# Norms in an fp32 kernel of two transformer blocks: token sums as columns, small reciprocals, TensorE turning them into rows

## The chip, the core and the metric

The kernel runs on one core of a Trainium2 chip. The metric is the device time of one execution in microseconds (us); the runs of the kernel before give 1356.03 us as their median.

## What is computed

Two blocks run one after the other on 256 tokens of 1024 features, all in float32. The first has two layers (FFN, mixer, FFN; the mixer is a short convolution in one and a three-branch attention in the other, with shared keys and values). The second has an even mixer (sparse attention and retention) and an odd mixer (differential and latent attention), each with a pre-norm and a post-norm. What the change touches is the root mean square norm, over the 1024 features of a token or over the 64 or 128 features of one head:

```python
def rms_norm(x, gain=None):
    xf = x.astype(jnp.float32)
    y = xf * lax.rsqrt(jnp.mean(xf * xf, axis=-1, keepdims=True) + NORM_EPS)
    if gain is not None:
        y = y * gain.astype(jnp.float32)
    return y.astype(x.dtype)

def head_group_norm(x):
    mu = jnp.mean(xf, axis=-1, keepdims=True)
    var = jnp.mean(jnp.square(xf - mu), axis=-1, keepdims=True)
    return ((xf - mu) * lax.rsqrt(var + NORM_EPS)).astype(x.dtype)
```

Such norms stand ahead of every FFN, mixer and projection (eight of them over 1024 features are touched), on the queries of the first attention (16 heads of 64), on the retention output (4 heads of 128, `head_group_norm`), on the differential attention output (4 heads of 128), and behind both mixers of the second block (post-norms).

## The kernel before

**Layout.** Activations lie with features on the 128 partitions and the 256 tokens along the free axis: `hres` holds the residual as 8 tiles of 128x256. One core runs everything; each engine has its own program, written by hand in the order in which it executes, and the engines meet at semaphores. A wait on an engine holds all that stands behind it there.

**Products.** Every large product is three TensorE matmuls (`mm3`, L744 to L746): weights and activations are each split into a high and a low fp32r part. Weights arrive in chunks (`raw_a`); ScalarE writes the high part (`hi_a`, L1225), VectorE the low part (`lo_a`, L1692, 128x2048 for a full chunk). The second matrix of an FFN, mixer or convolution comes by rows through `raw_b`, whose low part GpSimd makes (`low_quarters`, L2328, four 128x256 pieces a row tile).

**Deferred norm.** A stage does not wait for its norm. ScalarE writes the gained residual tiles (`gained`) and TensorE runs the first weight chunk on them (`first_chunk`, L733 to L738). Meanwhile ScalarE squares the residual, two tiles an instruction, into `sqm` (`square_residual`, L1319). `sum_pairs` (L713) then adds the eight 128x256 tiles of squares over partitions with a matrix of ones as stationary operand, so that every partition holds the sum of each token as a row of 256. ScalarE takes the root (`root_pairs`, L1341), VectorE inverts it (`inverse_rms`, L1682, 128x256) into `rln`, and the products are scaled by it when they leave PSUM. In a projection `turn_rms` (L723, two one-column matmuls after the second job) also turns it into a column per token half, `rtok`, for outputs with tokens on partitions.

**Order of work around the norms.** In a projection (`project`), job after job fills bank 4 or 5; after job 0 TensorE does the sum, and `between(c)` runs small extra work after chunk c. On ScalarE a chunk's end is followed by the high part of chunk c+2, then by `between(c)`; on VectorE by the scaling of the job, the low part of chunk c+2, then `between(c)`. At chunk 0 VectorE makes the low part of chunk 2 first and inverts after it. The even projection has 16 jobs, one a chunk; its `between` on VectorE holds the top-64 selection (`best`, rounds of MAX and MATCH_REPLACE) at chunks 8, 9, 11 and 12.

**Head norms.** `sum_squares` (L690) is one 512-column matmul of `sqs` against ones or `blk1` (ones in two 64x64 blocks), with rows as a result again. The inversion is of 128x512: in the q projection for two query pairs (L1675), inside the first attention in four pieces of 128x256 (`late_queries`, L2108), after the even attention (`group_root`, L2156) and after the odd attention (`c_norm`, L2292).

**Post-norms.** `post_residual` (from L1763): the four banks are squared by ScalarE, folded from 8 tiles to 4 by VectorE (L1770), summed by TensorE (`sum_residual`, L702), rooted (L1299), inverted (L1675) and multiplied in (L1783, or L1777 for the last one).

**Attention.** `attend` is a pipeline over pairs of heads: TensorE scores, VectorE maximum and bias, ScalarE exponential, VectorE and GpSimd scaling, TensorE transposes (L949 to L954) and values (L968 to L976). `mix_out` multiplies by the output matrix in `OUT_ORDER`; for the odd mixer the tiles of the second half come first.

## Time and profile before

| | us |
|---|---|
| median of 3 runs | 1356.03 (1355.47 to 1356.52) |
| span of the profiled execution, first to last instruction | 1354.7 |
| TensorE busy in it | 1302.7 (96%) |
| VectorE busy | 831.3 (61%) |
| ScalarE busy | 614.4 (45%) |
| GpSimd busy | 502.5 (37%) |

The page gives the profiled execution by its span; its own device time is not listed apart from the runs, whose median lies 1.3 us above the span. The mean granted TensorE clock is 0.980 of full speed. A matmul's listed duration contains its latency, so durations of matmuls that follow each other overlap: what one costs is read from the distance between starts. An fp32 matmul is listed as two instructions (x2), an fp32r one as one. ScalarE is ACT, VectorE DVE, GpSimd POOL, TensorE PE in the rows; "[0.74 <-ACT wah L1225]" means that the engine sat idle for 0.74 us until that line on that engine released it.

### The profile page before, as it was taken

The numbers are of one execution on the slowest core, as the hardware profiler recorded it, in microseconds if no ns is written. First come the engines' busy times: TensorE is split into PE (matmuls) and PEld (weight loads), VectorE is DVE, ScalarE is ACT, GpSimd is POOL, SyncE is SP. The second block draws the span as 40 slices with busy tenths as digits, with TensorE's granted clock in tenths as the row PEclk, the third lists the DMA queues.
The fourth block names the chain that finished last, engine by engine and source line by source line (L and its number), as shares of the span: only waits on it lengthen the run. The fifth ranks groups of instructions, "written<-read, shape, count | busy, mean of one in ns | idle before, by whom it ended". The sixth has DMA issues, their size and how long they took to land.

```text
span 1354.7 us, 27623 instructions
## 1 busy us (share of the span) xinstructions
PE 1302.7 (96%) x10767; PEld 1247.2 (92%) x10767; DVE 831.3 (61%) x1353; ACT 614.4 (45%) x880; POOL 502.5 (37%) x533
## 2 busy tenths in 40 slices
PE   8999999999999998999999889999999998989978
PEld 6999999999999998999999668999999997889768
DVE  4775557786555566554455785755556685875576
ACT  5444435344443345433335576534434346443382
POOL 2655443325444524455540244444442001700043
PEclk9999999999999998999998889999999999989989
DMA  8787754666776556666653114566653444334400
GB/s 257 211 234 220 219 171 141 187 187 207 228 231 187 171 162 176 199 186 187 197 160 129 56 48 130 173 200 197 199 177 121 156 139 181 112 95 133 148 32 32
DMA packets 275121, 222.61 MB, mean 164 GB/s; under 512 B 8098, under 2 KB 256438, under 8 KB 274924
## 3 DMA queue, kind: packets, MB, share of 16 engines
q1 hardware_dynamic: 272528, 215.59, 52.1%
q0 software_dynamic: 1504, 4.49, 1.7%
q10 hardware_dynamic: 1020, 1.58, 0.3%
q8 instruction: 47, 0.77, 0.2%
q14 instruction: 22, 0.18, 0.0%
HBM read 216.40 MB, written 4.19 MB: 163 GB/s over the span
## 4 chain that ended last, share of the span: by engine, by line
PE 83%; DVE 9%; ACT 4%; issue 1%; DMA 1%; POOL 1%; DVEq 0%; SPq 0%; ACTq 0%; POOLq 0%
PE psum L744 24%; PE psum L746 23%; PE psum L745 23%; PE psum L713 2%; PE psum L733 1%; PE psum L734 1%; DVE wal L1885 1%; PE psum L738 1%; DVE wal L1692 1%; ACT wah L1225 1%; PE psum L928 1%; DVE hn_tiles L1746 1%; ACT pbuf L1491 1%; DVE rstd L1675 1%; DVE hn_tiles L1745 1%
## 5 line engine op out<-in xcount | busy, mean ns | idle before, releaser
L744 PE MATMUL psum<-hn_tiles,wah 128*128 128x256 f32 x2032 | 570.4, 281 | 4.5 <-DVE wal L1692 2.4
L2328 POOL TENSOR_TENSOR wbl<-raw_b,wbh 128x256 fp32r<-128x256 f32 x412 | 402.0, 1005 | 465.6 <-ACT wbh L1232 443.0
L745 PE MATMUL psum<-hn_tiles,wah 128*128 128x256 f32 x2032 | 563.4, 277 | 0.0
L746 PE MATMUL psum<-hn_tiles,wal 128*128 128x256 f32 x2032 | 563.1, 277 | 0.0
L744 PEld LDWEIGHTS psum<-hn_tiles,wah 128*128 128x128 f32 x2032 | 382.4, 188 | 9.7 <-issue 4.7
L745 PEld LDWEIGHTS psum<-hn_tiles,wah 128*128 128x128 f32 x2032 | 381.9, 188 | 1.9 <-issue 1.7
L746 PEld LDWEIGHTS psum<-hn_tiles,wal 128*128 128x128 f32 x2032 | 382.1, 188 | 0.0
L1692 DVE TENSOR_TENSOR wal<-raw_a,wah 128x2048 fp32r<-128x2048 f32 (+3 forms) x127 | 288.9, 2274 | 111.5 <-ACT wah L1225 110.7
L1225 ACT ACTIVATE wah<-raw_a 128x2048 fp32r<-128x2048 f32 (+2 forms) x125 | 235.3, 1884 | 69.2 <-PE psum L746 54.9
L1351 ACT ACTIVATE gate_hid<-tmp 128x256 f32<-128x256 f32 x88 | 36.7, 417 | 415.3 <-DVE tmp L1802 415.3
L744 PE MATMUL psum<-hidh,wbh 128*128 128x256 f32 x768 | 212.6, 277 | 0.9 <-DVE hidl L1746 0.9
L745 PE MATMUL psum<-hidl,wbh 128*128 128x256 f32 x768 | 212.2, 276 | 0.0
L746 PE MATMUL psum<-hidh,wbl 128*128 128x256 f32 x768 | 212.1, 276 | 0.0
L1802 DVE TENSOR_TENSOR tmp<-psum,rms 128x512 f32<-128x512 f32 x88 | 60.8, 691 | 215.6 <-PE psum L746 208.7
L2397 POOL TENSOR_SCALAR pbuf<-pbuf,rs 128x256 f32<-128x256 f32 x36 | 35.8, 1004 | 319.5 <-DVE rs L1947 244.7
L744 PEld LDWEIGHTS psum<-hidh,wbh 128*128 128x128 f32 x768 | 144.2, 188 | 1.3 <-DVE hidl L1746 1.3
L746 PEld LDWEIGHTS psum<-hidh,wbl 128*128 128x128 f32 x768 | 144.2, 188 | 0.0
L745 PEld LDWEIGHTS psum<-hidl,wbh 128*128 128x128 f32 x768 | 144.2, 188 | 0.0
L1232 ACT ACTIVATE wbh<-raw_b 128x1024 fp32r<-128x1024 f32 x96 | 100.2, 1044 | 10.5 <-PE psum L746 6.1
L1806 DVE TENSOR_TENSOR gate_hid<-gate_hid,tmp 128x256 f32<-128x256 f32 x88 | 39.1, 444 | 43.6 <-ACT gate_hid L1351 43.6
L733 PE MATMUL psum<-hn_tiles,wah 128*128 128x256 f32 x144 | 40.2, 314 | 7.9 <-ACT hn_tiles L1305 4.3
L1746 DVE TENSOR_TENSOR hidl<-gate_hid,hidh 128x256 fp32r<-128x256 f32 x96 | 43.4, 452 | 3.4 <-DVE hidh L1745 0.2
(303 smaller groups left out, 1646.1 us busy)
## 6 DMA issues: line engine op xcount, KB each, us to landing
raw_a<-in_ffn_w_in SPq DMA_DIRECT2D x176, 512.0 KB, 5.0
raw_b<-in_ffn_w_out SPq DMA_DIRECT2D x88, 512.0 KB, 4.3
raw_a<-in_w_in_even SPq DMA_DIRECT2D x15, 1024.0 KB, 5.2
raw_a<-in_conv_w_in SPq DMA_DIRECT2D x24, 512.0 KB, 4.3
raw_a<-in_w_in_odd SPq DMA_DIRECT2D x11, 1024.0 KB, 5.2
raw_a<-in_w_kv SPq DMA_DIRECT2D x6, 1024.0 KB, 5.0
raw_b<-in_conv_w_out SPq DMA_DIRECT2D x8, 512.0 KB, 5.6
raw_a<-in_attn_w_q SPq DMA_DIRECT2D x4, 1024.0 KB, 5.3
```

Of the source, the lines that this page charges most:

```text
L733: mm(dst, wh, hnh[:, k, :], start=k == 0 and i == 0, stop=False)
L744: mm(dst, wh, xh, start=start, stop=False)
L745: mm(dst, wh, xl, start=False, stop=False)
L746: return mm(dst, wl, xh, start=False, stop=stop)
L1225: act.activation(wah[:, s, :, 0:w], raw_a[:, wa.slot(u), :, 0:w], ACT.Copy).then_inc(S("a_hi"), 1)
L1232: act.activation(wbh[:, s], raw_b[:, s], ACT.Copy).then_inc(S("b_hi"), 1)
L1351: act.activation(silu[:, gs, :], tmp[:, gs, 0:T], ACT.Silu).then_inc(S("silu_ready"), 1)
L1692: v.tensor_tensor(wal[:, s, :, 0:w], raw_a[:, (n["ra"] + u) % 2, :, 0:w], wah[:, s, :, 0:w].bitcast(F32), ALU.subtract).then_inc(S("a_lo"), 1)
L1746: return v.tensor_tensor(xl, x, xh.bitcast(F32), ALU.subtract)
L1802: v.tensor_tensor(tmp[:, gs, :].rearrange("p (g c) -> p g c", g=2), bank[4 + gs][:, :].rearrange("p (g c) -> p g c", g=2), rln[:, None, :] ...
L1806: link(v.tensor_tensor(hf[:, hs, :], silu[:, gs, :], tmp[:, gs, T:2 * T], ALU.mult))
L2328: x = g.tensor_tensor(low[:, c], full[:, c], high[:, c].bitcast(F32), ALU.subtract)
```

## The change

- **Token sums as columns.** `sum_tokens` makes the squares the stationary operand and one column of ones the moving one: per tile two fp32 matmuls with a one-column result, tokens on partitions. Eight tiles are folded to four before it, for the deferred norms by GpSimd (`fold_squares`).
- **Small roots.** ScalarE takes the root of 128x2, 128x4 or 128x8 (`rtt`), VectorE inverts as little (`token_roots`, `head_roots`). For tokens the result is `rtok` directly, and `turn_rms` with its copy goes.
- **Back to rows.** `rms_row` (two fp32 matmuls) and `head_rows` (four or eight) take the inverted column, broadcast over the free axis, as stationary operand and the identity as moving one; the rows land in PSUM. TensorE issues them after the twelfth matmul (k == 4) of the next job: in an FFN of the second chunk, in the convolution of its third group, in a projection of job 1; for heads of a later job (`amid`). VectorE copies the token rows to `rln`, or reads head rows from PSUM directly, and then signals `row_taken`, for which later TensorE work waits.
- **Head norms moved.** The late queries are scaled at attention steps 1 and 2; the retention norm is done at chunks 12 to 14 of the even projection instead of after the attention; the odd one at attention steps 10 and 11 and after it.

```diff
-def sum_residual():
-    pe.wait_ge(S("rt_ready"), n["rn"])
-    for j in range(4):
-        n["half"] += 1
-        pe.wait_ge(S("half_ready"), n["half"])
-        m = mm(bank[6][:, 0:T], one1, sqm[:, 2 * j, :], start=j == 0, stop=j == 3)
+def sum_tokens(b, tiles, ready):
+    pe.wait_ge(S("row_taken"), n["row"])
+    for j, t in enumerate(tiles):
+        ready(j)
+        for tt in range(2):
+            m = mm(b[:, tt:tt + 1], sqm[:, t, tt * P:(tt + 1) * P], one1[:, 0:1],
+                   start=j == 0 and tt == 0, stop=j == len(tiles) - 1 and tt == 1)
     m.then_inc(S("ss_ready"), 1)
     n["rn"] += 1
-    n["sqn"] += 4
+def half_tiles(j):
+    n["half"] += 1
+    pe.wait_ge(S("half_ready"), n["half"])
+def fold_tiles(j):
+    n["fold"] += 1
+    pe.wait_ge(S("fold_ready"), n["fold"])
+def sum_residual():
+    pe.wait_ge(S("rt_ready"), n["rn"])
+    sum_tokens(bank[6], range(0, KT, 2), half_tiles)
 def sum_pairs():
     pe.wait_ge(S("rt_ready"), n["rn"])
-    for j in range(4):
-        pe.wait_ge(S("sqn_ready"), n["sqn"] + j + 1)
-        for t in (2 * j, 2 * j + 1):
-            m = mm(bank[7][:, T:2 * T], one1, sqm[:, t, :], start=t == 0, stop=t == KT - 1)
+    sum_tokens(bank[7], range(0, KT, 2), fold_tiles)
+def rms_row(b):
+    n["tok"] += 1
+    pe.wait_ge(S("tok_ready"), n["tok"])
+    for tt in range(2):
+        m = mm(b[:, T + tt * P:T + (tt + 1) * P], rtok[:, tt:tt + 1].to_broadcast([P, P]), ident,
+               start=True, stop=True)
+    m.then_inc(S("row_ready"), 1)
+    n["row"] += 1
+def sum_head_tokens(b, src, per_tile):
+    n["sq"] += 1
+    pe.wait_ge(S("sq_ready"), n["sq"])
+    pe.wait_ge(S("row_taken"), n["row"])
+    col = halves2 if per_tile == 2 else one1[:, 0:1]
+    for t in range(2):
+        for tt in range(2):
+            c = per_tile * (2 * t + tt)
+            m = mm(b[:, c:c + per_tile], src[:, t * T + tt * P:t * T + (tt + 1) * P], col,
+                   start=True, stop=True)
     m.then_inc(S("ss_ready"), 1)
     n["rn"] += 1
-    n["sqn"] += 4
-def turn_rms():
-    n["tok"] += 1
-    pe.wait_ge(S("rms_ready"), n["tok"])
-    for tt in range(2):
-        m = mm(bank[7][:, T - 2 + tt:T - 1 + tt], rln[:, tt * P:(tt + 1) * P], ident[:, 0:1],
-               start=True, stop=True)
-    m.then_inc(S("tok_ready"), 1)
+def head_rows(b, slot, per_tile):
+    n["hrow"] += 1
+    pe.wait_ge(S("rh_ready"), n["hrow"])
+    for t in range(2):
+        for tt in range(2):
+            c = per_tile * (2 * t + tt)
+            w = P // per_tile
+            for j in range(per_tile):
+                m = mm(b[w * j:w * (j + 1), t * T + tt * P:t * T + (tt + 1) * P],
+                       rh[:, slot, c + j:c + j + 1].to_broadcast([P, w]), ident, start=True, stop=True)
+    m.then_inc(S("row_ready"), 1)
+    n["row"] += 1
...
+                if sums and i is FIRST and u == 1 and g == 0 and k == 4:
+                    rms_row(bank[7])
...
+                if i is FIRST and u == 0 and k == 4:
+                    rms_row(bank[7])
...
+                    if part == 0 and k == 4:
+                        rms_row(bank[7]) if idx == 1 else amid(idx)
...
+    pe.wait_ge(S("row_taken"), n["row"])
...
+    elif c == 1:
+        sum_squares(1, 60, blk1)
     else:
-        sum_squares(1, 60 if c == 1 else 512, blk1)
-project("q", q_between)
+        pe.wait_ge(S("rt_ready"), n["rn"])
+        sum_head_tokens(bank[6], sqs, 2)
+project("q", q_between, lambda idx: head_rows(bank[6], idx % 2, 2) if idx >= 3 else None)
 pe.wait_ge(S("nsa_in"), 1)
 pe.wait_ge(S("swap_kT"), 32)
 def nsa_between(st):
     if st == 1:
-        sum_squares(1, 512, blk1)
+        head_rows(bank[6], 1, 2)
+        sum_head_tokens(bank[7], sqs, 2)
+    elif st == 2:
+        head_rows(bank[7], 0, 2)
     elif st == 3:
-        pe.wait_ge(S("rt_ready"), n["rn"])
-    elif st in (12, 15, 18, 21):
-        pe.wait_ge(S("late_queries"), st // 3 - 3)
+        pe.wait_ge(S("row_taken"), n["row"])
...
-        sum_squares(1, 512, one1)
-project("even", even_between)
+        pe.wait_ge(S("rt_ready"), n["rn"])
+        sum_head_tokens(bank[6], sqs, 1)
+project("even", even_between, lambda idx: head_rows(bank[idx - 11], idx % 2, 1) if idx in (13, 14) else None)
 wait_scaled(pe, PJ["even"])
 wait_finished(pe, PJ["even"])
 pe.wait_ge(S("dsa_in"), 1)
 attend("even")
 mix_out("even")
 sum_residual()
+rms_row(bank[6])
...
-        sum_squares(1, 512, one1, (sqs[:, :], rstd[:, :])[st - 9], bank[st - 9])
+        sum_head_tokens(bank[st - 9], (sqs, rstd)[st - 9], 1)
+    if st == 11:
+        head_rows(bank[0], 0, 1)
 attend("odd", sum_heads)
+head_rows(bank[1], 1, 1)
 mix_out("odd")
 sum_residual()
+rms_row(bank[6])
...
+def head_roots(b, w, inv):
+    act.wait_ge(S("ss_ready"), n["rn"] + 1)
+    act.wait_ge(S("rt_used"), n["rn"])
+    act.activation(rtt[:, 0:w], b[:, 0:w], ACT.Sqrt, bias=eps[:, 0:1], scale=inv
                    ).then_inc(S("rt_ready"), 1)
     n["rn"] += 1
...
-def inverse_rms(tokens=False):
+def token_roots():
     v.wait_ge(S("rt_ready"), n["rn"] + 1)
-    link(v.reciprocal(rln, rt[:, 0:T]))
+    link(v.reciprocal(rtok, rtt[:, 0:2]))
     v.sem_inc(S("rt_used"), 1)
-    if tokens:
-        v.sem_inc(S("rms_ready"), 1)
+    v.sem_inc(S("tok_ready"), 1)
+    n["rn"] += 1
+def inverse_rms():
+    token_roots()
+    n["row"] += 1
+    v.wait_ge(S("row_ready"), n["row"])
+    link(v.tensor_copy(rln, bank[7][:, T:2 * T]))
+    v.sem_inc(S("row_taken"), 1)
+def head_roots(slot, w):
+    v.wait_ge(S("rt_ready"), n["rn"] + 1)
+    link(v.reciprocal(rh[:, slot, 0:w], rtt[:, 0:w]))
+    v.sem_inc(S("rt_used"), 1)
+    v.sem_inc(S("rh_ready"), 1)
     n["rn"] += 1
...
-    inverse_root(T)
+    token_roots()
+    n["row"] += 1
+    v.wait_ge(S("row_ready"), n["row"])
+    row = rstd[:, 0:T]
+    link(v.tensor_copy(row, bank[6][:, T:2 * T]))
+    v.sem_inc(S("row_taken"), 1)
...
 def normed_queries(j):
-    inverse_root(512)
+    n["row"] += 1
+    v.wait_ge(S("row_ready"), n["row"])
     qq = qT[:, 2 * j:2 * j + 2, :].rearrange("p t c -> p (t c)")
-    link(v.scalar_tensor_tensor(qq, qq, gq[:, 0:1], rstd[:, :], ALU.mult, ALU.mult))
+    link(v.scalar_tensor_tensor(qq, qq, gq[:, 0:1], bank[6 + j // 3][:, :], ALU.mult, ALU.mult))
+    v.sem_inc(S("row_taken"), 1)
 def q_between(c):
     if c == 1:
         inverse_root(60)
         link(v.scalar_tensor_tensor(kcT[:, :], kcT[:, :], gk[:, 0:1], rstd[:, 0:60], ALU.mult, ALU.mult))
-    elif c in (2, 3):
-        normed_queries(c - 2)
+    elif c in (2, 3, 4):
+        head_roots((c + 1) % 2, 8)
+        if c < 4:
+            normed_queries(c - 2)
 project("q", q_between)
 wait_finished(v, PJ["q"])
 def late_queries(st):
-    if st in (6, 9, 12, 15):
-        j, t = 2 + (st - 6) // 6, (st // 3) % 2
-        if t == 0:
-            v.wait_ge(S("rt_ready"), n["rn"] + 1)
-        link(v.reciprocal(rstd[:, 0:T], (rt if j == 2 else sqs)[:, t * T:(t + 1) * T]))
-        x = v.scalar_tensor_tensor(qT[:, 2 * j + t, :], qT[:, 2 * j + t, :], gq[:, 0:1], rstd[:, 0:T],
-                                   ALU.mult, ALU.mult)
-        link(x)
-        v.sem_inc(S("late_queries"), 1)
-        if t == 1:
-            v.sem_inc(S("rt_used"), 1)
-            n["rn"] += 1
+    if st == 1:
+        normed_queries(2)
+        head_roots(0, 8)
+    elif st == 2:
+        normed_queries(3)
...
 def group_norm(j):
     r2 = bqk[:, 2 * j:2 * j + 2, :].rearrange("p t c -> p (t c)")
     g2 = bg[:, 2 * j:2 * j + 2, :].rearrange("p t c -> p (t c)")
-    link(v.tensor_tensor(r2, r2, rstd[:, :], ALU.mult))
+    n["row"] += 1
+    v.wait_ge(S("row_ready"), n["row"])
+    link(v.tensor_tensor(r2, r2, bank[2 + j][:, :], ALU.mult))
+    v.sem_inc(S("row_taken"), 1)
     link(v.tensor_tensor(r2, r2, g2, ALU.mult))
...
     elif c == 12:
         best(0, range(HALF, 2 * HALF))
+        head_roots(1, 4)
+    elif c == 13:
+        wait_finished(v, PJ["q"] + 8)
+        group_norm(0)
+        head_roots(0, 4)
+    elif c == 14:
+        group_norm(1)
 project("even", even_between)
 wait_finished(v, PJ["even"])
 v.sem_inc(S("dsa_in"), 1)
-attend("even", behind=lambda st: group_root(0) if st == len(STAGES["even"]) else None)
+attend("even")
 for j in range(2):
-    if j:
-        group_root(j)
-    group_norm(j)
...
+def c_scaled(j):
+    n["row"] += 1
+    v.wait_ge(S("row_ready"), n["row"])
+    link(v.scalar_tensor_tensor(pair(cq, j), pair(cq, j), gsub[:, 0:1], bank[j][:, :], ALU.mult, ALU.mult))
+    v.sem_inc(S("row_taken"), 1)
+def c_gated(j):
+    link(v.scalar_tensor_tensor(pair(cq, j), pair(cq, j), 1.0 - LAM_INIT, pair(cg, j), ALU.mult, ALU.mult))
     for t in (2 * j, 2 * j + 1):
         x = split(hnh[:, t, :], hnl[:, t, :], cq[:, t, :])
     x.then_inc(S("tile_ready"), 1)
-attend("odd")
+def c_norm(st):
+    if st in (10, 11):
+        head_roots(st - 10, 4)
+    if st == 11:
+        c_scaled(0)
+attend("odd", behind=c_norm)
+c_scaled(1)
 for j in range(2):
-    c_norm(j)
+    c_gated(j)
...
+def fold_squares():
+    for j in range(4):
+        g.wait_ge(S("sqn_ready"), n["sqn"] + j + 1)
+        g.tensor_tensor(sqm[:, 2 * j, :], sqm[:, 2 * j, :], sqm[:, 2 * j + 1, :], ALU.add
+                        ).then_inc(S("fold_ready"), 1)
+    n["sqn"] += 4
```

The first place is VectorE at chunks 12 to 15 of the even projection, before the change (`L2175`, `L2176`, `L2179` and `L2180` are the last rounds of `best`, `wal` the low part of a chunk, `arena<-psum,rms` the scaling of a job):

```order
L2175 MAX top<-arena 128x8 [waits dve_link]
L2176 MATCH_REPLACE arena<-top,arena 128x128 [waits dve_link]
L2179 TENSOR_SCALAR arena<-arena 128x128 [waits dve_link]
L2180 TENSOR_TENSOR arena<-arena,cst 128x128 [waits dve_link]
L1692 TENSOR_TENSOR wal<-raw_a,wah 128x2048 [waits a_hi,dve_link]
L1736 TENSOR_TENSOR arena<-psum,rms 128x512 [waits a_lo,pj_ready]
L1736 TENSOR_TENSOR arena<-psum,rms 128x512 [waits pj_ready]
```

and after it:

```order
L2248 MAX top<-arena 128x8 [waits dve_link]
L2249 MATCH_REPLACE arena<-top,arena 128x128 [waits dve_link]
L2252 TENSOR_SCALAR arena<-arena 128x128 [waits dve_link]
L2253 TENSOR_TENSOR arena<-arena,cst 128x128 [waits dve_link]
L1757 RECIPROCAL rh<-rtt 128x4 [waits rt_ready,dve_link]
L1766 TENSOR_TENSOR wal<-raw_a,wah 128x2048 [waits dve_link,a_hi]
L2235 TENSOR_TENSOR arena<-arena,psum 128x512 [waits a_lo,row_ready,job_finished]
L2237 TENSOR_TENSOR arena<-arena 128x512 [waits dve_link]
L1757 RECIPROCAL rh<-rtt 128x4 [waits rt_ready,dve_link]
L1810 TENSOR_TENSOR arena<-psum,rms 128x512 [waits dve_link,pj_ready]
```

The small reciprocal stands behind the selection, and the first scaling by head rows (L2235) and the second reciprocal behind the low part of the last chunk.

The second place is TensorE there, after the change: the end of job 12, the sum of chunk 12 (L747), twelve matmuls of job 13 (two rows of the twelve shown last), then the head rows (L761), and, 36 matmuls later, the sum of chunk 13:

```order
L785 MATMUL psum<-wah,hn_tiles 128x256
L747 MATMUL psum<-cst,sqs 128x1 [waits row_taken,sq_ready,rt_ready]
L747 MATMUL psum<-cst,sqs 128x1 x3
L783 MATMUL psum<-wah,hn_tiles 128x256 [waits job_scaled,a_lo]
...
L784 MATMUL psum<-wal,hn_tiles 128x256
L785 MATMUL psum<-wah,hn_tiles 128x256
L761 MATMUL psum<-cst,rh 128x128 [waits rh_ready]
L761 MATMUL psum<-cst,rh 128x128 x3
L783 MATMUL psum<-wah,hn_tiles 128x256
...
L747 MATMUL psum<-cst,sqs 128x1 [waits row_taken,sq_ready,rt_ready]
```

Before, one L690 stood for each sum, and nothing in job 13 or 14 waited for VectorE's reciprocals.

The third place is VectorE at the end of the odd attention after the change (L2066 multiplies a head pair by its gate, L1819 and L1820 split it, L2373 is the scaling by head rows):

```order
L1757 RECIPROCAL rh<-rtt 128x4 [waits rt_ready]
L2066 TENSOR_TENSOR arena<-psum,arena 128x256 [waits dve_link,job_finished,pv_done]
L1819 CAST hn_tiles<-arena 128x256 [waits o_evac]
L1820 TENSOR_TENSOR hn_tiles<-arena,hn_tiles 128x256 [waits dve_link]
L1757 RECIPROCAL rh<-rtt 128x4 [waits rt_ready]
L2373 SCALAR_TENSOR_TENSOR arena<-arena,par,psum 128x512 [waits dve_link,row_ready]
L2066 TENSOR_TENSOR arena<-psum,arena 128x256 [waits dve_link,job_finished,pv_done]
L1819 CAST hn_tiles<-arena 128x256 [waits o_evac]
L1820 TENSOR_TENSOR hn_tiles<-arena,hn_tiles 128x256 [waits dve_link]
L2373 SCALAR_TENSOR_TENSOR arena<-arena,par,psum 128x512 [waits row_ready]
```

Before, both reciprocals (of 128x512) and both scalings stood behind the last split, and `mix_out` did not wait for them; now its first matmul waits for `row_taken`, the signal behind the last L2373.

## Rows read from the trace of the kernel before

**Rows 1.** Share and count of each engine's busy time (page, part 1)

```profile
PE 1302.7 (96%) x10767; PEld 1247.2 (92%) x10767; DVE 831.3 (61%) x1353; ACT 614.4 (45%) x880; POOL 502.5 (37%) x533
```

**Rows 2.** TensorE timeline, kv projection: start us, us, engine line op out<-in xcount

```profile
487.37 3.62 PE L713 MATMUL psum<-arena,cst 128*128 128x256 f32 x16
...
490.64 0.47 PE L744 MATMUL psum<-hn_tiles,wah 128*128 128x256 f32 x1
```

**Rows 3.** Groups by line, TensorE: xcount | busy us, mean ns | idle before

```profile
L1202 PE MATMUL psum<-cst,arena 128*128 128x128 f32 x32 | 3.7, 275 | 0.0
...
L723 PE MATMUL psum<-cst,rms 128*128 128x1 f32 x16 | 2.6, 266 | 0.2 <-DVEq L1685 0.2
```

**Rows 4.** Timeline, GpSimd, at the start of the convolution stage

```profile
210.40 4.85 POOL L2328 TENSOR_TENSOR wbl<-raw_b,wbh 128x256 fp32r<-128x256 f32 x4 [12.34 <-ACT wbh L1232]
```

**Rows 5.** Timeline, ScalarE and VectorE, kv projection

```profile
483.81 2.19 ACT L1319 ACTIVATE arena<-hres 128x512 f32<-128x512 f32 x4
...
492.00 1.75 DVE L1682 RECIPROCAL rms<-rt 128x256 f32<-128x256 f32 x1
```

**Rows 6.** Timeline, TensorE and VectorE, convolution stage

```profile
209.09 3.62 PE L713 MATMUL psum<-arena,cst 128*128 128x256 f32 x16
...
214.79 1.75 DVE L1682 RECIPROCAL rms<-rt 128x256 f32<-128x256 f32 x1
```

**Rows 7.** Timeline, TensorE and VectorE, q projection

```profile
741.60 1.02 PE L690 MATMUL psum<-sqs,cst 128*128 128x512 f32 x2
...
743.75 2.29 DVE L1692 TENSOR_TENSOR wal<-raw_a,wah 128x2048 fp32r<-128x2048 f32 x1 [1.18 <-ACT wah L1225]
```

**Rows 8.** Timeline, TensorE, first attention: two pairs of 64-row matmuls

```profile
778.36 0.39 PE L976 MATMUL psum<-ptb,arena 128*64 128x128 f32 x4
...
778.67 0.62 PE L934 MATMUL psum<-lamj,arena 64*128 64x15 f32 x8
```

**Rows 9.** Timeline, TensorE and VectorE, end of the even projection

```profile
1120.51 1.02 PE L690 MATMUL psum<-sqs,cst 128*128 128x512 f32 x2
...
1123.45 2.29 DVE L1692 TENSOR_TENSOR wal<-raw_a,wah 128x2048 fp32r<-128x2048 f32 x1 [0.74 <-ACT wah L1225]
...
1129.02 0.29 DVE L2180 TENSOR_TENSOR arena<-arena,cst 128x128 f32<-128x128 f32 x1
```

**Rows 10.** Groups by line, VectorE: a reciprocal of four columns, a scaling of 128x512

```profile
L1953 DVE RECIPROCAL rs<-sm 128x4 f32<-128x4 f32 x24 | 4.2, 176 | 3.7 <-ACT pbuf L1491 1.8 <-ACT tmp L1491 1.7
...
L2163 DVE TENSOR_TENSOR arena<-arena,rstd 128x512 f32<-128x512 f32 x2 | 2.4, 1220 | 0.1
```

**Rows 11.** Timeline, TensorE and VectorE, post-norm after the even mixer

```profile
1186.06 1.75 DVE L1675 RECIPROCAL rstd<-rt 128x256 f32<-128x256 f32 x1 [1.30 <-ACT rt L1299]
1187.97 0.48 DVE L1783 SCALAR_TENSOR_TENSOR tmp<-psum,par,rstd 128x256 f32<-128x256 f32 x1 [0.16 <-DVE rstd L1675]
...
1189.66 0.55 PE L733 MATMUL psum<-hn_tiles,wah 128*128 128x256 f32 x1 [4.14 <-ACT hn_tiles L1305]
```

**Rows 12.** Timeline, ScalarE and TensorE, end of the last attention

```profile
1316.24 1.28 ACT L1279 ACT_TABLE_LOAD   x1
...
1318.85 0.39 PE L744 MATMUL psum<-hn_tiles,wbh 128*128 128x256 f32 x1 [1.71 <-ACT sqs L1279]
```

**Rows 13.** Timeline, TensorE and GpSimd, end of the even attention

```profile
1158.83 0.65 PE L974 MATMUL psum<-ptb,arena 128*64 128x256 f32 x4 [1.09 <-DVE arena L1987]
...
1160.52 13.46 POOL L2328 TENSOR_TENSOR wal<-raw_a,wah 128x256 fp32r<-128x256 f32 x16
```

**Rows 14.** Windows: span, busy us (x) of PE, PEld, DVE, ACT, POOL; PEclk, DMA, GB/s

```profile
1189.00:1192.00 3.00, 2.17 (x9) 1.91 (x9) 2.93 (x7) 1.70 (x4) 0.00 (x0) 0.50 0.00 0
1195.00:1198.00 3.00, 3.00 (x25) 3.00 (x24) 3.00 (x8) 2.43 (x6) 0.00 (x0) 0.90 0.00 0
...
728.00:732.00 4.00, 4.00 (x21) 4.00 (x20) 0.14 (x1) 0.00 (x0) 0.00 (x0) 0.50 1.07 402
```

**Rows 15.** Chain of waits in order of time, first attention: start us, us, what

```profile
798.31 1.76 DVE rstd L2108
```

95 lines of the change are left out of this document (46 added, 49 removed).

## Prediction

> **What bounds the kernel.** I read the page first: TensorE is busy for 96% of the span [rows 1], so a wait moved onto it is paid in full, and time saved on another engine is worth nothing unless TensorE waited for it. Then its timeline at each norm, for starts rather than durations; then VectorE's and ScalarE's beside it, to see when a small reciprocal could be ready; then the clock.
>
> At a deferred norm TensorE does not wait now. Its sum starts at 487.37 and the next product at 490.64 [rows 2]: 3.27 us for eight fp32 matmuls of 256 columns. The reciprocal of 1.75 us starts at 492.00 [rows 5] and is hidden by those products. So the long reciprocals are mostly off the path, and the question is where the new rows make TensorE wait for VectorE.
>
> **Prices.** An fp32 matmul (two listed) of 128 columns costs 3.7 / 16 = 0.23 us [rows 3]. For one column the lower end is half of that, 0.12, if one of the two parts were hidden; it can't be nothing, since two instructions are still issued. The upper end is 2.6 / 8 = 0.33, pairs that stand alone with their latency [rows 3]. I take 0.2: eight in a stream are nearer to the row of 32 than to the lone pairs. A row pair of `rms_row` is 0.46. Two matmuls with 64 output rows each take 778.67 - 778.36 = 0.31 [rows 8], so eight of them in `head_rows` 1.3; the four with 128 output rows 0.9. A small reciprocal is 0.18 [rows 10]; I add 0.1 for the semaphore to TensorE.
>
> **1. Deferred norms, eight.** Before: 8 x 3.27, and 2.6 for the four `turn_rms` [rows 2, 3], 28.8 in all. The new sum has eight one-column matmuls, 1.6, but also waits for GpSimd's folds. ScalarE's four squares span 483.81 to 486.00 [rows 5], so the first ends some 3.0 before TensorE asks and the last 1.4 before. A GpSimd operation of 128x256 takes 13.46 / 16 = 0.84 [rows 13] to 4.85 / 4 = 1.2 [rows 4]; I take 1.0. Folds one after the other then end 1.0 after TensorE asks, the last two matmuls come behind, and the sum ends between 1.6 and 2.2; I take 1.7.
>    - Three FFNs: VectorE inverts before anything else, so the column is there when twelve matmuls (1.4) have passed. 1.7 + 0.46 = 2.2, against 3.27: -3.3 together.
>    - Four projections: VectorE makes a low part first, so its reciprocal can't start before 492.00, 4.63 after the sum began [rows 2, 5]. With 0.28 for it and the semaphore, 0.46 for the rows, less 1.4 of products done meanwhile, TensorE spends 4.0 each. In the q projection 0.8 of other small matmuls fills part: 15.2 in all, where 13.1 + 2.6 stood: -0.5.
>    - The convolution: the reciprocal starts 5.70 after the sum [rows 6], which makes 5.0, against 3.27: +1.8.
>    - Sum -2.0.
>
> The Trainium skill (Advanced Engine Details and Errata, GPSIMD Details) says that GpSimd shares a read and a write interface with VectorE when a VectorE instruction has two SBUF inputs. That is a rule against putting the folds beside VectorE's low parts. By it each fold would be at the slow end and each FFN sum 0.5 later, 1.5 us in all; the row of the convolution [rows 4] shows that value with VectorE at work, so the trace agrees in part, and I leave this to the range.
>
> **2. Post-norms, two.** From the reciprocal's start to the first multiplication is 1187.97 - 1186.06 = 1.9 now [rows 11]. After: 0.18 + 0.1, two matmuls and their latency 0.7, a copy from PSUM of about 0.4 and its wait 0.15: 1.5. The root on two columns saves about 0.2 more. -0.6 each: -1.2.
>
> **3. Query norms in the projection.** Job 2 ends where L690 starts, 741.60. VectorE makes a low part from 743.75 for 2.29 [rows 7]; only behind it stands the reciprocal, so the rows can start at about 746.4. TensorE gets there at 741.60 + 0.8 (four small matmuls) + 1.45 = 743.85: it waits 2.5. For job 4 no low part stands ahead and I see no wait. Three sums cost 0.35 more each than the 0.45 of L690, two `head_rows` 1.3 each. 2.5 + 1.05 + 2.6, less 0.55 of a wait for VectorE at the attention's start: +5.6.
>
> **4. First attention.** Two more `head_rows` at its start, with scores queued behind them on TensorE and the first maxima behind the scaling on VectorE: +2.3 after slack. Of the four late reciprocals one, with its scaling, is on the chain of waits, 1.76 from 798.31 and 0.5 behind it [rows 15]; the others end beside TensorE work. -2.3. Net 0.
>
> **5. Retention norm in the even projection: the large term.** Job 12 ends at 1120.51 [rows 9]. ScalarE takes the root early enough. But VectorE has the low part from 1123.45 to 1125.74, which can't start earlier since its high part waits for job 12, and then the second half of the selection until 1129.31; the small reciprocal stands behind that. The rows can start at 1129.6. TensorE asks at 1120.51 + 0.8 + 1.45 = 1122.8: a wait of 6.8. Then job 13 ends, and the sum of chunk 13 waits for `row_taken`: the scaling by the first rows stands behind the low part of chunk 15. By the distances just read that part ends 5.2 after the job's end, and 1.2 for a 128x512 scaling [rows 10], somewhat less when it reads PSUM without GpSimd beside it, makes 6.1. Sums and rows add 2 x 0.35 + 2 x 0.9 = 2.5. +15.4. Nothing covers this: TensorE is in order and all of job 13, 14 and 15 is queued behind.
>    Behind the attention VectorE loses two reciprocals of 3.35 and both scalings. TensorE's wait of 1.09 for an evacuation [rows 13] goes. More doesn't: GpSimd's low parts run from 1160.52 for 13.46 [rows 13] and are late next. -1.2.
>
> **6. Odd attention.** ScalarE's table load starts at 1316.24 and takes 1.28 [rows 12]; it needs the last probabilities' copy before it, so the first small root ends at about 1317.7. VectorE waits there in order, with the next evacuation (until 1319.5) queued behind, then the second reciprocal, the first scaling (1.1), the last evacuation and split (1.4), the second scaling (1.1): 1323.7. `mix_out` now waits for that, where it starts at 1318.85 now [rows 12]: +4.9, less 0.6 of a later wait for a low part that VectorE now makes in time. +4.3.
>
> **7. The clock.** After the idle 4.14 us before 1189.66 [rows 11] the granted clock is 0.50 (1.2 GHz), and 0.90 on average in 1195 to 1198 [rows 14]: half rate until about 1195.6, which costs half of 5.9, 2.9. Both waits of step 5 are longer than that idle time: +5.8.
>
> Sum: -2.0 - 1.2 + 5.6 + 0 + 15.4 - 1.2 + 4.3 + 5.8 = +26.7. On the profiled span 1354.7 this gives 1381.4. The median of the runs is 1.3 above that span; with it the forecast is **1382.7**.
>
> The row from 728 to 732 shows 0.50 with TensorE busy for all 4.00 us, with small matmuls [rows 14]: the clock can fall without idle time. I count nothing for the norms, where 1.6 us of one-column matmuls, 1.4 of products and 1.8 of waiting follow each other. The Trainium skill (TensorE: Matmul & The Clock Gate, HAM oscillation) lays the fall to idle gaps; by it 5.8 stands as it is. The row says that more is possible, rival B.
>
> **Rivals.**
> - **A. The waits are covered, and it is faster.** If VectorE reached its small reciprocals before TensorE's twelfth matmul everywhere, the norms would cost 8 x 2.16 = 17.3 instead of 28.8, -11.5; with posts -1.2, queries +3.1, the even projection +2.5, its attention -1.2, the odd one -0.6: -8.9, 1347. The place is the even projection, and it decides at 2.3 us after job 12's end. For it: VectorE is busy for 61%. Against it: the order of instructions puts a low part and half the selection in front, and the part starts 2.9 after the job's end [rows 9]. Chance 0.05.
> - **B. The clock falls at five norms too** (convolution and projections), 2.9 each less some overlap, +12: 1395. For it the row of 728; against it the 1.4 us of dense products inside. 0.17.
> - **C. The first attention gains.** Half-rate stretches there come back earlier with VectorE freed of all four reciprocals, 4 x 2.25 = 9, and the late waits of step 6 are half as long: 1372. For it: late queries hold scores; against: only one is on the chain. 0.15.
> - **D. No measurable difference**: the gains of A everywhere but in step 5, whose waits cancel them. 0.02. That the rows or folds are not in the program is ruled out by its order.
>
> **Numbers.** My forecast has 0.61. A measurement tells about 0.2%, 2.7 us, from no change. Range: down to C and a bit, up to B: with the 112 one-column matmuls off by up to 0.1 either way, 11 us at most, 1367 to 1397; A, D and what lies beyond C and B are left out. Faster 0.05, same 0.02, slower 0.93.
>
> **What would show it.** TensorE waiting twice in the even projection, about 6.8 before L761 and 6.1 before L747, for VectorE; one wait of 2.5 in the q projection; 1.8 at each L733 of a projection and 2.8 in the convolution; none in the FFNs; first L783 of the odd `mix_out` released by the second L2373; clock 0.5 behind the two long waits. The forecast is wrong if those two are under 2 us, or if L705's sums take over 2.5.

## The result, and the profile after

The changed kernel takes 1394.97 us (median of 4 runs, 1393.74 to 1396.23) against 1356.28 us of the kernel before in the same comparison: ratio 1.0287, 95% interval 1.0274 to 1.0299. It is slower by 39 us. The forecast was 1382.7 with a range of 1367 to 1397: the sign and the range hold, the size falls short by 12 us. The profiled execution has a span of 1393.0 us, 38.3 above that of before.

The page of the changed kernel, part 1, answers to [rows 1]:

```profile
span 1393.0 us, 28056 instructions
...
PE 1321.4 (95%) x10951; PEld 1272.5 (91%) x10951; DVE 807.1 (58%) x1359; ACT 606.8 (44%) x876; POOL 533.7 (38%) x565
```

VectorE lost 24 us of work and GpSimd gained 31, and neither total decides the time. TensorE's busy time grew by 19 us although its sums became shorter, and 20 us of idle time came on top. Since matmuls at half rate are listed longer (0.41 us in place of 0.28), "busy" hides one of the causes.

To see where the time went I took the start of the same product in both TensorE timelines, place by place; the difference grows where a kernel loses and shrinks where it gains. The table has these steps in us for the changed kernel and for two experiments told below; the last row is the whole difference of the spans. Each column is one profiled execution; how far two executions of one kernel can lie apart at a place is told with e8 and e10.

| place | forecast | changed | e5, wide sums | e9, all mended |
|---|---|---|---|---|
| start-up, ahead of any change | 0 | +0.5 | -1.2 | +0.5 |
| norm of the first FFN | -1.1 | -1.5 | -1.5 | -1.5 |
| norm of the convolution | +1.8 | +1.5 | +1.4 | +1.5 |
| norm of the second FFN | -1.1 | +2.1 | +0.5 | +0.5 |
| norms of four projections: kv, q, even, odd | -0.5 | +1.6, +1.1, +1.0, +0.6 | +0.4, +0.1, +1.0, +0.6 | +0.2, +0.3, +1.1, +0.6 |
| norm of the third FFN | -1.1 | +1.4 | -0.2 | -0.1 |
| query norms in the q projection | +5.6 | +7.4 | +7.4 | +0.7 |
| first attention | 0 | -5.2 | -5.2 | -0.1 |
| retention norm in the even projection | +21.2 | +20.4 | +20.7 | +1.9 |
| even attention | -1.2 | -2.2 | -1.6 | -1.6 |
| first post-norm | -0.6 | 0.0 | -0.4 | -0.4 |
| odd projection and attention | 0 | +1.1 | -0.4 | -0.5 |
| end of the odd attention | +4.3 | +5.3 | +5.2 | +0.4 |
| last post-norm and output | -0.6 | +3.1 | +1.5 | +0.5 |
| whole span | +26.7 | +38.3 | +28.2 | +4.2 |

(21.2 is 15.4 of step 5 and 5.8 of step 7.) The start-up differs by up to 1.7 us between profiled executions, whatever the kernel; a span carries this, the steps don't.

**The two long waits came as forecast.** TensorE timeline of the changed kernel, even projection, where [rows 9] stood; the last brackets give the idle time ahead and what ended it:

```profile
1130.36 0.95 PE L747 MATMUL psum<-cst,sqs 128*128 128x1 f32 x8
1139.59 2.08 PE L761 MATMUL psum<-cst,rh 128*128 128x128 f32 x8 [6.77 <-DVEq L1759]
1153.75 1.84 PE L747 MATMUL psum<-cst,sqs 128*128 128x1 f32 x8 [6.11 <-DVEq L2236]
1158.16 1.49 PE L761 MATMUL psum<-cst,rh 128*128 128x128 f32 x8
```

6.77 and 6.11 us were 6.8 and 6.1 in step 5. VectorE's timeline there shows what stood ahead of the first reciprocal (low part, last rounds of the selection) and of the first scaling (a low part):

```profile
1133.31 2.29 DVE L1766 TENSOR_TENSOR wal<-raw_a,wah 128x2048 fp32r<-128x2048 f32 x1 [0.75 <-ACT wah L1277]
...
1137.90 0.29 DVE L2248 MAX8 top<-arena 128x8 f32<-128x128 f32 x1
...
1139.21 0.18 DVE L1757 RECIPROCAL rh<-rtt 128x4 f32<-128x4 f32 x1
1150.35 2.29 DVE L1766 TENSOR_TENSOR wal<-raw_a,wah 128x2048 fp32r<-128x2048 f32 x1 [10.97 <-ACT wah L1277]
1152.86 0.69 DVE L2235 TENSOR_TENSOR arena<-arena,psum 128x512 f32<-128x512 f32 x1 [0.22 <-DVE wal L1766]
```

**The clock fell at the deferred norms too, with little or no idle time first.** Windows of the changed kernel (columns as in [rows 14]; the third number from the end is the granted clock): around the kv norm, whose sum starts at 490.30, around the first query rows, in the first attention, and behind the two long waits.

```profile
490.00:493.00 3.00, 2.35 (x20) 2.30 (x21) 2.85 (x2) 2.14 (x3) 0.50 (x1) 1.00 0.00 0
493.00:497.00 4.00, 3.54 (x19) 3.24 (x19) 2.39 (x3) 0.00 (x0) 0.00 (x0) 0.57 0.80 271
...
753.00:757.00 4.00, 4.00 (x24) 4.00 (x23) 0.39 (x1) 0.00 (x0) 0.00 (x0) 0.59 0.54 203
770.00:778.00 8.00, 7.16 (x52) 6.22 (x52) 4.01 (x20) 3.67 (x11) 0.00 (x0) 0.58 0.01 2
1139.00:1142.00 3.00, 2.41 (x11) 2.41 (x12) 0.35 (x2) 0.00 (x0) 0.00 (x0) 0.50 1.01 403
1142.00:1146.00 4.00, 4.00 (x23) 4.00 (x23) 0.00 (x0) 0.00 (x0) 0.00 (x0) 0.57 0.04 11
```

Read in windows of 2 us, the norms of convolution, second FFN, kv, third FFN and even projection, and the last post-norm, are each followed by a stretch in which 1.7 us are lost: the granted clock is 0.50 (1.2 GHz) for some 3.4 us. In the kernel before it is 1.00 in all six. In the convolution and the even projection TensorE has no idle time of more than 0.1 us ahead of the fall (TensorE timeline), in the others 0.6 to 1.4 us. In the q projection, where the clock falls in the kernel before too, the stretch starts sooner behind the sum and is 3.4 us longer (0.54 over 728 to 743, where before it is 0.57 over 727 to 739). In the first FFN the clock stays at 1.00 in both of these executions.

**GpSimd's folds slow VectorE.** Groups by line, VectorE, low tiles: the kernel before, then the changed one.

```profile
L1710 DVE SCALAR_TENSOR_TENSOR hn_tiles<-hres,par,hn_tiles 128x256 fp32r<-128x256 f32 x72 | 29.3, 479 | 0.1
```

```profile
L1784 DVE SCALAR_TENSOR_TENSOR hn_tiles<-hres,par,hn_tiles 128x256 fp32r<-128x256 f32 x72 | 39.0, 611 | 0.1
```

The eight low tiles of a stage take 3.25 us before and 4.70 now in six stages, and 4.22 in the second FFN. There it works the other way too: the folds take 1.4 us each (GpSimd's timeline), and TensorE stands in the middle of its sum for them (TensorE's timeline, below):

```profile
301.83 5.55 POOL L2411 TENSOR_TENSOR arena<-arena 128x256 f32<-128x256 f32 x4 [12.32 <-ACT arena L1369]
```

```profile
304.64 1.39 PE L705 MATMUL psum<-cst,arena 128*128 128x1 f32 x12
307.43 0.61 PE L705 MATMUL psum<-cst,arena 128*128 128x1 f32 x4 [1.40 <-POOL arena L2411]
```

**The end lost its cover.** TensorE timelines of the kernel before and of the changed one. L1196, now L1248, transposes the residual for the output; L1202 (L1254) adds the normed tiles.

```profile
1343.77 3.73 PE L1196 MATMUL psum<-cst,hres 128*128 128x128 f32 x32
1347.34 3.74 PE L1202 MATMUL psum<-cst,arena 128*128 128x128 f32 x32
```

```profile
1377.23 1.92 PE L705 MATMUL psum<-cst,arena 128*128 128x1 f32 x16
1379.86 0.71 PE L733 MATMUL psum<-cst,rms 128*128 128x128 f32 x4 [0.71 <-DVEq L1743]
1380.40 5.37 PE L1248 MATMUL psum<-cst,hres 128*128 128x128 f32 x32
1385.61 3.74 PE L1254 MATMUL psum<-cst,arena 128*128 128x128 f32 x32
```

Before, the transposes ran while VectorE inverted. Now they stand behind the row matmuls, and run partly at half rate: 5.2 us in place of 3.6. So two things cost time here, the order and the clock; e2, e5 and e9 tell them apart.

### The profile page after: what moved, and what is told of

Read it like the earlier page. It is cut to its first block, busy times and chain, and to the rows that moved or that the text cites. A ratio compares the mean times of both kernels' runs of the same rounds, so it can differ in the third digit from the quotient of the medians.

```text
span 1393.0 us, 28056 instructions
## 1 busy us (share of the span) xinstructions
PE 1321.4 (95%) x10951; PEld 1272.5 (91%) x10951; DVE 807.1 (58%) x1359; ACT 606.8 (44%) x876; POOL 533.7 (38%) x565
## 4 chain that ended last, share of the span: by engine, by line
PE 83%; DVE 8%; ACT 5%; issue 2%; POOL 1%; DMA 0%; DVEq 0%; SPq 0%; ACTq 0%; POOLq 0%
PE psum L783 24%; PE psum L784 24%; PE psum L785 24%; DVE wal L1766 2%; ACT wah L1277 1%; DVE hn_tiles L1784 1%; ACT pbuf L1546 1%; PE psum L1016 1%; DVE wal L1964 1%; PE psum L761 1%; PE psum L705 1%; PE psum L772 1%; PE psum L733 1%; PE psum L970 1%; PE psum L773 1%
## 5 line engine op out<-in xcount | busy, mean ns | idle before, releaser
L783 PE MATMUL psum<-hn_tiles,wah 128*128 128x256 f32 x2032 | 574.1, 283 | 5.4 <-DVE wal L1766 3.1
L783 PEld LDWEIGHTS psum<-hn_tiles,wah 128*128 128x128 f32 x2032 | 386.6, 190 | 10.3 <-issue 5.9
L784 PEld LDWEIGHTS psum<-hn_tiles,wah 128*128 128x128 f32 x2032 | 386.4, 190 | 1.0 <-issue 1.0
L785 PEld LDWEIGHTS psum<-hn_tiles,wal 128*128 128x128 f32 x2032 | 386.6, 190 | 0.0
L1766 DVE TENSOR_TENSOR wal<-raw_a,wah 128x2048 fp32r<-128x2048 f32 (+3 forms) x127 | 292.3, 2302 | 115.4 <-ACT wah L1277 114.2
L783 PE MATMUL psum<-hidh,wbh 128*128 128x256 f32 x768 | 212.5, 277 | 0.9 <-DVE hidl L1820 0.9
L783 PEld LDWEIGHTS psum<-hidh,wbh 128*128 128x128 f32 x768 | 144.2, 188 | 1.1 <-DVE hidl L1820 1.1
L2411 POOL TENSOR_TENSOR arena<-arena 128x256 f32<-128x256 f32 x32 | 34.5, 1105 | 95.2 <-ACT arena L1369 95.2
```

The costliest lines, as they stand in the source:

```text
L783: mm(dst, wh, xh, start=start, stop=False)
L784: mm(dst, wh, xl, start=False, stop=False)
L785: return mm(dst, wl, xh, start=False, stop=stop)
L1766: v.tensor_tensor(wal[:, s, :, 0:w], raw_a[:, (n["ra"] + u) % 2, :, 0:w], wah[:, s, :, 0:w].bitcast(F32), ALU.subtract).then_inc(S("a_lo"), 1)
```

## The experiments

**e1: the even projection's rows one job later.** TensorE's part and VectorE's part of the edit:

```diff
-project("even", even_between, lambda idx: head_rows(bank[idx - 11], idx % 2, 1) if idx in (13, 14) else None)
+project("even", even_between, lambda idx: head_rows(bank[idx - 12], (idx - 1) % 2, 1) if idx in (14, 15) else None)
...
+    head_roots(1, 4)
     best(0, range(HALF, 2 * HALF))
-    head_roots(1, 4)
 elif c == 13:
+    head_roots(0, 4)
+elif c == 14:
     wait_finished(v, PJ["q"] + 8)
     group_norm(0)
-    head_roots(0, 4)
-elif c == 14:
+elif c == 15:
     group_norm(1)
```

> The changed kernel (1395) with the even projection's head rows one job later, its first small reciprocal ahead of the second half of the selection, its first scaling one chunk later; nothing is computed otherwise. My theory: the 20.4 us that TensorE loses between jobs 12 and 15 are the waits of 6.77 and 6.11 before L761 and L747 with the half-rate stretch behind each (2.9 each), and 2.5 of sums and rows. Then both waits are under 0.5 us, the clock stays at 1.0 there, and the time falls by 17 to 18, to about 1377. Rival: VectorE is the bound of these chunks (low parts and selection), and only moves the wait: then TensorE waits elsewhere in jobs 13 to 15 or at the start of the attention, and it falls by under 10, to 1385 or more.

Measured: 1374.6 us, ratio to before 1.0147 (1.0128 to 1.0166), 20.4 less than the changed kernel. By place the even projection costs +1.9 instead of +20.4. No matmul there has an idle time ahead of it any more (TensorE's timeline), and VectorE's first reciprocal comes before the rounds of the selection:

```profile
1129.42 0.95 PE L747 MATMUL psum<-cst,sqs 128*128 128x1 f32 x8
1135.98 0.95 PE L747 MATMUL psum<-cst,sqs 128*128 128x1 f32 x8
1138.26 1.05 PE L761 MATMUL psum<-cst,rh 128*128 128x128 f32 x8
1144.73 1.05 PE L761 MATMUL psum<-cst,rh 128*128 128x128 f32 x8
```

```profile
1134.81 0.18 DVE L1757 RECIPROCAL rh<-rtt 128x4 f32<-128x4 f32 x1
```

```profile
1128.00:1140.00 12.00, 12.00 (x106) 12.00 (x105) 9.85 (x31) 7.50 (x10) 0.00 (x0) 1.00 0.92 333
```

The window shows the clock at 1.00 with TensorE busy throughout. The theory holds, and the rival (VectorE is the bound, the wait only moves) does not: VectorE does the same work, and the loss was the order, that is, where its two small reciprocals stood and how early TensorE asked for the rows. The time fell by more than the 17 to 18 expected: 18.5 us are at this place, and about 1.5 are the profiled execution's shorter start-up, which is not the edit's doing.

**e2: the end and the odd mixer.** The last row behind three groups of transposes, and the odd head rows inside `mix_out`, in banks 6 and 7 (VectorE's scalings both behind the attention, as before the change):

```diff
 sum_residual()
-rms_row(bank[6])
...
     if Y_BANK[j] == 6:
+        rms_row(bank[6])
...
-    if st == 11:
-        head_rows(bank[0], 0, 1)
 attend("odd", sum_heads)
-head_rows(bank[1], 1, 1)
-mix_out("odd")
+mix_out("odd", lambda i: head_rows(bank[4 + i], i - 2, 1) if i in (2, 3) else None)
```

> The changed kernel with two moves read apart by place. (1) End: the row matmuls of the last post-norm stand behind twelve of the sixteen residual transposes (L1248) instead of ahead of all. Theory: TensorE loses 3.0 at the end because these 5.2 us of transposes, which ran while VectorE inverted, now wait for the row; then this gives back 3 to 3.6. Rival: the loss is the clock's half rate at 1381 to 1384 alone, which stays if the waits stay: under 1.5. (2) Odd mixer: both head rows come inside mix_out, in banks 6 and 7, and it does not wait for VectorE's scalings. Theory: the 5.5 us lost there are that wait (forecast 4.3); it gives back 4 to 5.5. Rival: the output matrix's low parts or the last tiles are late next, under 2. Together by theory 1386 to 1388, by the rivals 1392 or more.

Measured: 1388.9 us, ratio 1.0242 (1.0224 to 1.0259), 6.1 less than the changed kernel. `mix_out` now starts without the wait for VectorE's scalings (changed kernel, then e2, TensorE's timelines):

```profile
1353.22 0.36 PE L783 MATMUL psum<-hn_tiles,wbh 128*128 128x256 f32 x1 [2.12 <-issue]
```

```profile
1349.27 0.39 PE L783 MATMUL psum<-hn_tiles,wbh 128*128 128x256 f32 x1 [1.33 <-ACT rtt L1398]
1354.83 1.05 PE L761 MATMUL psum<-cst,rh 128*128 128x128 f32 x8
```

By place the odd mixer gives back 4.9, as expected; 1.7 of that is the clock, 0.58 in 1353 to 1357 in the changed kernel and 1.00 in e2. The end gives back only 1.7, less than the 3 expected, and this is all clock: it is 1.00 in e2 from 1373 on, and 0.66 in 1380 to 1385 in the changed kernel. e5 below, with the old order and the clock at 1.00, costs as much there (+1.5) as e2 (+1.4). Behind three groups the row comes too late: the last group waits 0.57 us for VectorE's copy of it. e9 has it behind one group.

**e3: no folds, all eight tiles summed as columns.**

```diff
-sum_tokens(bank[7], range(0, KT, 2), fold_tiles)
+sum_tokens(bank[7], range(KT), square_tiles)
...
-fold_squares()
```

> The changed kernel with no folds on GpSimd: TensorE sums all eight tiles as columns, sixteen one-column fp32 matmuls a norm, 3.4 us instead of 1.7. Theory F (folds beside VectorE): VectorE's eight low tiles (L1784), 3.25 us before and 4.70 now in projections and convolution, are slow because GpSimd folds at the same time; they come back to 3.25, and the low part of the weights behind them to its old time, so VectorE's small reciprocal is 1.5 to 2 us earlier in five stages. The time is then 13 longer for the matmuls and 8 to 10 shorter for this: 1397 to 1400. Theory C (clock): what the deferred norms lost (7.8 us where I forecast a gain of 2.0) is the half rate behind the one-column sums; low tiles matter little, the half-rate stretches stay or grow, and the time is 1405 or more.

Measured: 1409.18 us, ratio 1.0400 (1.0382 to 1.0418). Theory C gave 1405 or more, F 1397 to 1400: C is nearer. But what F says of the low tiles is so. They are back at their old mean:

```profile
L1785 DVE SCALAR_TENSOR_TENSOR hn_tiles<-hres,par,hn_tiles 128x256 fp32r<-128x256 f32 x72 | 29.3, 477 | 0.1
```

The total cannot say what this was worth. By place the eight norms cost some 12 us more than in the changed kernel, where 64 more matmuls of 0.21 take 13.7; the half-rate stretches at five norms are 3.4 us longer or new, up to 1.7 lost in each; and 3.4 more are in the first attention, which this edit leaves alone. With sixteen one-column matmuls the clock also falls behind the first FFN's sum, where the changed kernel kept 1.00, with TensorE busy all the time:

```profile
23.00:26.00 3.00, 3.00 (x29) 3.00 (x28) 0.00 (x0) 0.79 (x2) 2.51 (x4) 1.00 1.08 341
26.00:30.00 4.00, 4.00 (x25) 3.82 (x25) 0.17 (x1) 2.52 (x3) 0.26 (x1) 0.68 1.02 365
```

Sixteen in place of eight does not explain it. e2 has the first FFN of the changed kernel unaltered, with eight such matmuls, and in its execution the clock falls there too, again with TensorE busy throughout:

```profile
26.00:30.00 4.00, 4.00 (x23) 4.00 (x23) 1.14 (x3) 3.68 (x4) 0.46 (x1) 0.60 0.94 324
```

**e4: the kernel before, with the folds alone.**

```diff
 for j in range(4):
-    pe.wait_ge(S("sqn_ready"), n["sqn"] + j + 1)
-    for t in (2 * j, 2 * j + 1):
-        m = mm(bank[7][:, T:2 * T], one1, sqm[:, t, :], start=t == 0, stop=t == KT - 1)
+    n["fold"] += 1
+    pe.wait_ge(S("fold_ready"), n["fold"])
+    m = mm(bank[7][:, T:2 * T], one1, sqm[:, 2 * j, :], start=j == 0, stop=j == 3)
```

> The kernel before (1356) with one part of the change alone: GpSimd folds the squares from eight tiles to four and TensorE sums four tiles with 256 columns each, as rows, 1.64 us instead of 3.27; root, long reciprocal and all else as before. By theory C (only the clock behind one-column sums spoils the norms) folds are free: the clock stays at 1.0, and all eight norms gain 1.6 each, 1343. By theory F the low tiles of VectorE are 4.70 instead of 3.25 in the projections and the convolution, and TensorE waits for them or for the folds: it gives back 1 to 2 in six of eight norms, 1350 to 1356.

Measured: 1352.08 us, ratio 0.9974 (0.9962 to 0.9985): within F's 1350 to 1356, far from C's 1343. The clock behind the sums is as in the kernel before, but for the odd projection. The low tiles have 610 ns again:

```profile
L1710 DVE SCALAR_TENSOR_TENSOR hn_tiles<-hres,par,hn_tiles 128x256 fp32r<-128x256 f32 x72 | 39.0, 610 | 0.1
```

By place: first FFN -1.7, q projection -2.3, kv -0.8, third FFN -0.6, even -0.5, convolution -0.3, second FFN +0.1, odd projection +2.7; some 2 more are gained in the first attention, which e4 leaves alone. Halving TensorE's sum saves 1.6 a norm on paper. In convolution, kv, third FFN and even projection TensorE now waits 0.56 to 0.61 us behind the sum (in kv, for VectorE's low part of the weights), where it did not wait before; in the second FFN it waits 1.45 us for a fold. In the odd projection it waits 1.86 us for VectorE at `turn_rms`, where it was 0.22 before, and the clock is half rate behind that wait (TensorE's timeline, then a window):

```profile
1197.46 0.61 PE L723 MATMUL psum<-cst,rms 128*128 128x1 f32 x4 [1.86 <-DVEq L1685]
```

```profile
1200.00:1204.00 4.00, 4.00 (x24) 4.00 (x23) 0.42 (x1) 1.34 (x1) 0.00 (x0) 0.62 0.02 4
```

**e5: token sums with 128 columns.**

```diff
-m = mm(b[:, tt:tt + 1], sqm[:, t, tt * P:(tt + 1) * P], one1[:, 0:1],
+m = mm(b[:, tt * P:(tt + 1) * P], sqm[:, t, tt * P:(tt + 1) * P], one1,
```

> The changed kernel (1395) with one thing altered: the token sums multiply the squares by all 128 columns of ones instead of by one, same eight fp32 matmuls a norm, column 0 of each half used as before. By rows of before an fp32 matmul of 128 columns takes 0.23 us, a one-column one took 0.21 here, so the sums themselves cost the same within 0.2. Theory: the half-rate stretch of 3.4 us behind each sum (granted clock 0.50, 1.7 us lost; not there in the kernel before, and not with e4's 256-column sums) follows on TensorE doing almost only one-column matmuls; it goes, and with it 1.7 each in the convolution, second FFN, kv, third FFN, even projection and at the end: about 10, 1385. Rival: it follows on the waits around the sum (for folds, for the small reciprocal), which stay: 1395, clock 0.50 as before.

Measured: 1385.72 us, ratio 1.0205 (1.0182 to 1.0228), 9.3 less than the changed kernel (8.4 by place; the start-up of the profiled execution was 1.7 shorter). The sum takes 0.1 longer in its row, and behind it the clock holds. TensorE's timeline around the kv norm, then windows over the same stretch:

```profile
486.80 1.95 PE L705 MATMUL psum<-cst,arena 128*128 128x128 f32 x16
492.09 0.71 PE L733 MATMUL psum<-cst,rms 128*128 128x128 f32 x4 [1.16 <-DVEq L1743]
```

```profile
487.00:490.00 3.00, 2.46 (x22) 2.30 (x21) 2.85 (x2) 2.06 (x2) 0.00 (x0) 1.00 0.00 0
490.00:494.00 4.00, 2.84 (x24) 2.64 (x24) 2.75 (x4) 0.00 (x0) 0.00 (x0) 1.00 0.91 306
```

The wait for VectorE's reciprocal is longer here (1.16 us; 0.46 in the changed kernel) and the clock does not fall; in the convolution it does not even behind a wait of 2.30. The traces of all twelve runs together say the same. Leaving out the q projection, seven deferred norms stand in each. With one-column sums (the changed kernel, e1, e2, e3) the clock falls within 5 us of the sum's start in 23 of 28 places, not in the same ones each time: e2 has it in the first FFN and not in the third. With 128 or 256 columns (the kernel before and the seven other runs) it does so in none of 56; the one fall in e4's odd projection comes later, behind the wait of 1.86. So the falls at the norms came with the one-column sums, not with the waits.

**e6 and e7: the kernel before with the head norms alone.** Query norms as in the change, the retention norm as in e1, all else as before; e7 has the query rows 24 matmuls later:

```diff
-if part == 0 and k == 4:
+if part == half and k == 4:
     amid(idx)
...
-project("q", q_between, lambda idx: head_rows(bank[6], idx % 2, 2) if idx >= 3 else None)
+project("q", q_between, lambda idx: head_rows(bank[6], idx % 2, 2) if idx >= 3 else None, 1)
```

> The kernel before (1356) with the head norms of the change alone: query norms as the change has them, the retention norm as in e1 (rows one job later), odd mixer, token sums, folds and post-norms as before. Theory: by the places in the changed kernel and e1, q projection +7.3 (wait 2.6, its half rate, sums and rows), first attention -5.2, even projection +1.9, even attention -2.1 to -3: 1356 to 1358, no difference or little. Rival: what the first attention gained in the changed kernel came from its other parts (the clock falling earlier in the q projection), and heads alone lose 4 to 6: 1361.

> e6 with the head rows of the q projection 24 matmuls later (second half of the job instead of its fifth k of the first half). Theory: the wait of 2.56 before L761 and the 2.3 us of half rate behind it are due to the rows being asked for before VectorE is past its low part; both go, 4 to 5 us less than e6, 1352. Rival: VectorE's scaling behind the rows is then late for the next sum or for the attention's first scores, under 2 less.

Measured: e6 1361.96 us, ratio 1.0031 (1.0020 to 1.0041); e7 1358.22, 1.0005 (0.9996 to 1.0015). e6's theory (no difference) is wrong, its rival's 1361 right: q projection and first attention cost +4.9 together, where the changed kernel has +2.2. e7 gives back 3.7, short of the 4 to 5 expected: the wait of 2.56 stands in e6, but no half rate behind it (clock 1.00 in 747 to 758), so there was none to give back. The rest is the first attention. Windows over its half-rate stretches, in the kernel before, e6 and e7:

```profile
762.00:773.00 11.00, 9.79 (x52) 6.75 (x52) 8.00 (x38) 7.55 (x29) 5.95 (x6) 0.53 0.28 71
785.00:793.00 8.00, 7.20 (x40) 4.79 (x42) 6.64 (x26) 5.26 (x19) 3.52 (x4) 0.57 0.22 52
```

```profile
761.00:773.00 12.00, 9.93 (x73) 8.57 (x73) 4.97 (x21) 4.42 (x13) 0.00 (x0) 0.57 0.00 1
775.00:783.00 8.00, 6.58 (x30) 4.42 (x32) 4.69 (x28) 4.87 (x17) 4.05 (x5) 0.57 0.21 51
```

```profile
759.00:779.00 20.00, 18.41 (x114) 13.48 (x112) 11.08 (x58) 11.26 (x39) 5.95 (x6) 0.57 0.16 41
```

Length times what is missing to full clock: 5.2 + 3.4 = 8.6 us before, 5.2 + 3.4 = 8.6 in e6, 8.6 in e7, and 3.4 in the changed kernel (770 to 778; the 1.6 of 753 to 757 lie in its q projection). So about 5 of the 5.2 us that its first attention gains are less time at half rate. The head norms themselves don't bring it, since e6 and e7 lack it.

**e8 and e10: e4 without the folds of the second FFN and of the odd projection.** Those two norms sum eight tiles as rows, as before.

```diff
+n["norm"] += 1
+whole = n["norm"] in (3, 8)
```

> e4 (1352) without GpSimd's folds in the second FFN's norm (where TensorE waited for them) and in the odd projection's (where e4 lost 2.7). Theory: low tiles of 4.70 us are on the path only where the first chunk waits for them, above all in the odd projection, and the folds pay in the first FFN and the q projection: 1349. Rival: the 2.7 in the odd projection is not the folds' doing: 1352.

> e8 again with more rounds, to have its ratio closely: 1348 to 1351, ratio 0.994 to 0.997 with both ends below 1. If e8's gain was start-up noise of its runs, the interval reaches 1.

Measured: e8 1351.48 us, ratio 0.9959 (0.9938 to 0.9980); e10, the same kernel, 1350.42, 0.9947 (0.9929 to 0.9965). The first median is nearer to the rival's 1352 than to the 1349 of the theory, but the place speaks for the theory: the odd projection is at -0.3 and 0.0 instead of +2.7, without the wait of 1.86 and the half rate behind it. So that loss was the folds' doing. This version is 0.4 to 0.5% faster than the kernel before.

The two are also the only pair of traces of one and the same kernel, and they show how far the clock can move a place without any edit. Windows over the first attention, e8 and then e10:

```profile
756.00:783.00 27.00, 23.48 (x174) 16.03 (x172) 22.32 (x95) 19.37 (x71) 14.02 (x14) 0.81 0.23 59
```

```profile
756.00:783.00 27.00, 23.18 (x156) 15.68 (x158) 20.24 (x96) 17.15 (x63) 12.04 (x12) 0.75 0.17 45
```

That is 5.1 us lost against 6.8. In the q projection it is 3.4 (0.66 over 722 to 732) against 5.2 (0.57 over 722 to 734). By place the two executions are 3.9 us apart over q projection and first attention, 3.5 of it by these numbers, and the whole spans are 3.8 apart. So a difference of up to 4 us there, between two kernels read from one execution each, is not shown to be the kernels'. In e3 the first attention loses 8.6 us at half rate (0.61 over 774 to 796), in the changed kernel, e1, e2 and e5 3.4.

**e9: all places mended at once.** The edits of e1, e5, of e2's odd mixer and of e7, and the last row behind one group of transposes.

> The changed kernel with all its mended places together: even head rows one job later (e1, -18.5 by place), token sums with 128 columns (e5, about -10), odd head rows inside mix_out (e2, -4.9), query rows half a job later (-4 to -5 between e6 and e7), and the last row behind one group of the residual transposes instead of three (e2 had three and lost 1.4 against the kernel before; here -3.5). If these are the causes and separate, the sum is -41 on 1395: 1353 to 1355, no different from the kernel before or a little faster. Rival: part of them is one cost counted twice (half-rate stretches that come back elsewhere once a wait is gone): 1360 or more, over 0.3% slower than before.

Measured: 1359.1 us, ratio 1.0020 (1.0008 to 1.0032). 36 of the 39 us come back, less than the 41 of the expectation; the time lies between the theory's 1353 to 1355 and the rival's 1360. The table shows where: even projection 18.5, end of the odd attention 4.9 and last norm 2.6 are there, but e5's 10 are 8.4 by place, 1.6 of them at the end and so counted twice, and q projection with first attention gain only 1.6, not 4 to 5 (+0.6 where the changed kernel has +2.2), because half rate that the changed kernel is spared in the first attention comes back. The rival's idea, one cost counted twice, holds for the first of these two items; the second is within what e8 and e10 differ by.

## Why the prediction was right in sign and short in size

- **Step 1, deferred norms: -2.0 forecast, +7.8 measured; the largest miss.** The sum itself is right: eight one-column matmuls take about 1.7 us between starts. The size that failed is in step 7, "I count nothing for the norms": the clock falls behind five of the eight sums, 1.7 us each, and in the q projection the stretch that stood there before is 3.4 us longer. e5 takes 5.5 of the 9.8 back. Rival B had this mechanism and gave the measured time, 1395, but partly by luck: it put it at 2.9 in convolution and four projections, and it is 1.7, in two FFNs as well, and not in the odd projection. Another part of the miss is the folds. I took 1.0 each; they take 0.86 to 0.92 in six stages, 1.4 in the second FFN, where the sum waits 1.4 for one and takes 3.4 in all (over the 2.5 that I had named as a sign of being wrong), and 2.0 in the first. The 1.5 us that I left to the range were for the folds alone; I had them change nothing for VectorE, while the low tiles became 1.45 longer in six stages. The waits at L733 were forecast at 1.8 for a projection and 2.8 for the convolution. They are 0.46 (kv), 0.55 (q), none (even), 1.67 (odd) and 1.00. Where the clock falls, half-rate products fill part of them: with the clock held in e5 the kv wait is 1.16, the even one 1.23 and that of the convolution 2.30.
- **Step 2, post-norms: -1.2 forecast, +3.1 measured.** The first gains nothing; the clock is at half rate 3.4 us longer there than before. At the last I priced VectorE's chain alone and did not ask what TensorE did meanwhile: the residual transposes were hidden there, and the row matmuls now stand ahead of them. That was to be seen in the program's order. The order costs some 1.5 (e5, with the clock at 1.00) and the clock the other 1.6. e9 has it at +0.5.
- **Step 3, query norms: +5.6 forecast, +7.4 measured.** The wait is 2.56 for 2.5. Missing is the half rate behind it, 0.59 in 753 to 757: 1.6 us.
- **Step 4, first attention: 0 forecast, -5.2 measured.** Rival C had the effect, less time at half rate, and gave it 9. Its mechanism, VectorE freed of the four reciprocals, is not borne out: e6 and e7 free it as well and show none of it. About 5 of the 5.2 us is clock, and e8 and e10 show that this can differ between executions of one kernel, so calling the forecast of 0 right or wrong here is beyond these traces.
- **Step 5 and 7, even projection: +21.2 forecast, +20.4 measured.** Right part by part, and e1 shows the cause by removing it. Sums and rows cost 1.9 for 2.5.
- **Step 6, odd attention: +4.3 forecast, +5.3 measured.** The wait for `row_taken` is there, 2.12 us ahead of the first L783; the profile names no releaser, but that matmul starts 0.16 us behind the end of the second L2373. Missing are the wait of 2.04 ahead of the first head rows (L761), for the small root and reciprocal, and the half rate behind, 0.58 in 1353 to 1357: 1.7 us. e2 moves both rows and takes all three away, so it does not tell them apart.
- **Rival A** failed as the order said: in the even projection VectorE had a low part and the selection ahead of the small reciprocal. e1 shows that a change of order alone removes those waits, and e9 that even then the change gains nothing over the kernel before.

The Trainium skill (TensorE: Matmul & The Clock Gate, HAM oscillation), by which the clock falls at idle gaps, fits the even projection, where 0.50 follows both waits. It does not cover the falls at the norms: in the first FFN of e2 and e3 TensorE was busy throughout, and in e5 waits of 1.16 and 2.30 us were followed by 1.00. The rule on the interface shared by GpSimd and VectorE (Advanced Engine Details and Errata, GPSIMD Details) agrees with the traces: the low tiles, with two inputs in SBUF, go from 479 to 611 ns beside the folds and back to 477 without.

What stays open: whether the shorter half rate of the first attention belongs to the changed kernel or to its executions (the changed kernel, e1, e2 and e5 have it, e3 does not); why the clock falls behind a one-column sum in some executions and not in others, as in the first and third FFN; what the slower low tiles cost by themselves; and why the odd projection and attention vary by 1.5 us between kernels that are alike there.

## What to carry to other kernels

- A long vector operation that is hidden costs nothing. Before shortening it, list what the short form makes the busiest in-order engine wait for, and what stands ahead on the engine that answers. Here two such places, the even projection and the end of the odd attention, cost 20 and 5 of the 39 us. Another order of the small reciprocals and their rows gave back 18.5 and 4.9 of them.
- When a wait ahead of a fixed block of independent work is made shorter or moved, check that the independent work still fills it.
- Price tiny matmuls together with the clock of what follows them: look at the granted clock in windows of 2 us behind every such group.
- Before a difference of a few us at one place is put down to an edit, read the granted clock there in more than one execution: e8 and e10, the same kernel, differ by 3.9 us over two stages.

## What the runs showed of the hardware

- An fp32 sum of eight one-column matmuls (1.84 us listed) was followed by some 3.4 us at 1.2 GHz in six places of the changed kernel; in e2's first FFN (eight) and e3's (sixteen) no idle time stood ahead of the fall. The same sum with 128 columns (e5, 1.95 us) or, folded, with 256 (e4) was followed by full clock within 5 us, the q projection left out. For one fp32 matmul of 128x128 stationary, one column costs as much as 128, 0.21 to 0.23 us.
- A VectorE operation with two inputs in SBUF beside GpSimd folds took 611 ns for 479 in the mean (658 in the six stages concerned), and a fold 0.86 to 0.92 us in six stages, 1.4 in the second FFN and 2.0 in the first.
- Two executions of one kernel (e8, e10) had TensorE at half rate for 17 and 24 us in q projection and first attention together, and 3.8 us between their spans.
